# Summing a dense expert sweep in eights: eight keys per PSUM bank instead of four, on one core

## What is computed

```python
# 512 tokens; 16384 experts = 128 x 128 keys; 8 heads x 16 experts per token
act = gelu(einsum('td,ted->te', h, u_emb[expert])) * gate
out = einsum('te,ted->td', act, v_emb[expert])      # d = 2048
y   = rmsnorm(x + ga2 * out, g_final)
```

## Time and profile before

| what | value |
|---|---|
| runs of the kernel before | 3456.78, 3446.84, 3457.04 us; median 3456.78 us |
| span of the profiled execution | 3458.3 us (no other time is given for it) |
| PE, DVE, ACT, POOL busy over the span | 98%, 68%, 29%, 52% |
| chain that ended last | PE 88%, DVE 7%, the rest 5% |
| granted TensorE clock, mean | 0.990 of full speed |
| evictions `acc<-acc,bank` (L1962) | 372, 251.5 us busy |

### The profile page before, as it was taken

How to read it: one execution, slowest core, us unless ns; L and a number is a source line. 1 busy time by engine, 2 the same in 40 slices (tenths; PEclk the granted TensorE clock), 3 DMA queues, 4 the chain that set the end, 5 groups by cost and what they waited for, 6 DMA issues and landing times.

```text
span 3458.3 us, 44792 instructions
## 1 busy us (share of the span) xinstructions
PE 3376.2 (98%) x16931; PEld 2936.1 (85%) x16931; DVE 2361.7 (68%) x3848; ACT 1012.7 (29%) x1160; POOL 1805.8 (52%) x904
## 2 busy tenths in 40 slices
PE   6999999999999999999999999999999999999998
PEld 3688888766788889999999999999888888888886
DVE  2278887755514659994888888764667776767666
ACT  3332211143223232223222222223333323233233
POOL 1220000212544446676666666667777777778764
PEclk8999999999999999999999999999999999999999
DMA  8656642564424226777677777788988888888872
GB/s 337 265 186 205 216 168 94 191 245 175 194 96 152 90 105 248 265 278 275 257 314 302 281 282 299 305 314 313 377 327 329 317 325 328 316 326 324 321 277 97
DMA packets 184619, 874.72 MB, mean 253 GB/s; under 512 B 16621, under 2 KB 77501, under 8 KB 97844
## 3 DMA queue, kind: packets, MB, share of 16 engines
q1 hardware_dynamic: 122160, 525.38, 42.0%
q0 software_dynamic: 38688, 281.15, 20.1%
q10 hardware_dynamic: 23652, 66.69, 5.1%
HBM read 803.78 MB, written 69.32 MB: 252 GB/s over the span
## 4 chain that ended last, share of the span: by engine, by line
PE 88%; DVE 7%; DMA 1%; POOL 1%; issue 1%; ACT 1%; ACTq 0%; DVEq 0%; SPq 0%; POOLq 0%
PE bank L2080 82%; PE bank L2336 2%; PE bank L2452 1%; DMA ring<-in_w_mod 1%; PE bank L2310 1%; DVE b L1845 1%; PE bank L2088 1%; POOL low L769 1%; DVE rows_a L1784 1%; DVE b L1825 0%; DVE rows_c L1784 0%; PE bank L2436 0%; DVE tiny L1840 0%; DVE rows_b L1784 0%; DVE low L1403 0%
## 5 line engine op out<-in xcount | busy, mean ns | idle before, releaser
L811 POOL TENSOR_TENSOR split<-ring,split 128x1024 fp32r<-128x1024 f32 x544 | 1303.9, 2410 | 542.4 <-ACT split L1146 540.4
L2080 PE MATMUL bank<-h_hi,split 128*128 128x384 f32 (+1 forms) x4608 | 1221.8, 341 | 8.3 <-POOL split L811 7.0
L1146 ACT ACTIVATE split<-ring 128x1024 fp32r<-128x1024 f32 x544 | 577.8, 1063 | 1608.7 <-PE bank L2080 1588.3
L2080 PE MATMUL bank<-split,a_split 128*128 128x512 f32 x4608 | 1045.0, 389 | 0.1
L2080 PEld LDWEIGHTS bank<-split,a_split 128*128 128x128 f32 x4608 | 865.1, 188 | 179.8 <-POOL split L811 0.5
L2080 PEld LDWEIGHTS bank<-h_hi,split 128*128 128x128 f32 x4608 | 839.7, 188 | 29.7 <-POOL split L811 8.9
L2080 PE MATMUL bank<-h_lo,split 128*128 128x384 f32 (+1 forms) x2304 | 785.5, 341 | 0.0
L1962 DVE TENSOR_TENSOR acc<-acc,bank 128x512 f32<-128x512 f32 x372 | 251.5, 683 | 289.7 <-PE bank L2080 288.7
L2080 PEld LDWEIGHTS bank<-h_lo,split 128*128 128x128 f32 x2304 | 433.6, 188 | 9.5
L2080 PE MATMUL bank<-hT_hi,w_hi 128*128 128x512 f32 (+1 forms) x768 | 290.5, 378 | 8.5 <-DVE hT_lo L1408 4.4
L2080 PE MATMUL bank<-hT_lo,w_hi 128*128 128x512 f32 (+1 forms) x768 | 288.2, 375 | 0.0
(11 more groups left out here) (315 smaller groups left out, 3787.3 us busy)
## 6 DMA issues: line engine op xcount, KB each, us to landing
ring<-in_u_emb SPq DMA_DIRECT2D x128, 1024.0 KB
ring<-in_v_emb SPq DMA_DIRECT2D x128, 1024.0 KB
ring<-in_w_mod SPq DMA_DIRECT2D x48, 1024.0 KB
ring<-in_w_in SPq DMA_DIRECT2D x44, 1024.0 KB
ring<-in_w_mod SPq DMA_DIRECT2D x64, 512.0 KB, 4.7
neurons<-tiny ACTq DMA_DIRECT2D x128, 192.0 KB
gate_table<-b ACTq DMA_DIRECT2D x6, 4096.0 KB, 14.7
weigh<-neurons SPq DMA_DIRECT2D x32, 768.0 KB
```

The lines of the kernel that those rows point to most:

```text
L811: nc.gpsimd.tensor_tensor(split[:, r % 2, 1, at].bitcast(F32R), ring[:, r % 4, :, :].rearrange("p k n -> p (k n)")[:, at], split[:, r % 2, ...
L1146: nc.scalar.activation(split[:, q % 2, 0, at].bitcast(F32R), ring[:, q, :, :].rearrange("p k n -> p (k n)")[:, at], ACT.Copy)\
L2080: last = mm(out_, left[a].bitcast(F32R), right[b].bitcast(F32R), start=start and n == 0, stop=stop and n == 2)
```

## The change

A unit's place in the order changes: eight units now are two key groups by four column quarters, unit = 8i + k, group 2i + k % 2, quarter k // 2. A bank is begun by the even unit and finished by the odd one, with 24 matmuls, so DVE empties it only in odd units (192 flushes and merges instead of 384 of them). Both places of `a_split` are now read in turn in all eight units. ACT makes the first one of the next eight after unit 6 and the second after unit 7, and DVE's `rest_group` stands at the head of units 7 and 0; `weigh_group` stands in units 5 and 6. SP's two weigh loads stand ahead of units 2 and 4, each behind a wait for the `rest_group` of the place's old group. In the first eight units groups 2 and 3 are loaded ahead of units 4 and 6. Two small tensors of the row-by-row part (`h2_last`, `nval_last`) move to other places in SBUF.

```diff
@@ SyncE
-            def v_load(unit, group, q):
+            def v_load(unit, group, k):
                 sp.wait_ge(split_made, unit * 2 + 2 * (V0 - 3))
-                sp.dma_start(ring[:, q, :, :].rearrange("p k n -> p (k n)"),
-                             v_t[bass.ds(group, 1), q, :, :].rearrange("g p n -> p (g n)"))\
-                  .then_inc(quarter_full[q], 16)
+                sp.dma_start(ring[:, k % 4, :, :].rearrange("p k n -> p (k n)"),
+                             v_t[bass.ds(group, 1), k // 2, :, :].rearrange("g p n -> p (g n)"))\
+                  .then_inc(quarter_full[k % 4], 16)
...
-                    if k == 2 and not first:
-                        sp.wait_ge(a_split_made, i * 2)
-                        weigh_load(i * 2 + 1, 1)
-                    if k == 6 and not last:
-                        sp.wait_ge(a_split_made, i * 2 + 1)
-                        weigh_load(i * 2 + 2, 0)
-                    v_load(i * 8 + k, i * 2 + k // 4, k % 4)
+                    if k in (2, 4) and not last:
+                        sp.wait_ge(a_split_made, i * 2 + k // 2)
+                        weigh_load(i * 2 + 1 + k // 2, k // 2 - 1)
+                    v_load(i * 8 + k, i * 2 + k % 2, k)
...
             for k in range(4, 8):
-                if k == 6:
-                    sp.wait_ge(a_split_made, 1)
-                    weigh_load(2, 0)
-                v_load(k, 1, k % 4)
+                if k % 2 == 0:
+                    sp.wait_ge(a_split_made, k // 2 - 1)
+                    weigh_load(k // 2, k // 2 - 2)
+                v_load(k, k % 2, k)
@@ ScalarE
-                if k == NK - 2:
-                    a_hi(0, 0)
+                if k >= NK - 2:
+                    a_hi(k - NK + 2, k - NK + 2)
                 neurons(k, k % 4)
...
             with act.Fori(1, GROUPS // 2 - 1) as i:
                 for k in range(8):
+                    if k == 0:
+                        a_hi(1, i * 2 + 1)
+                    if k == 7:
+                        a_hi(0, i * 2 + 2)
                     sweep_unit(i * 8 + k, k % 4)
-                    if k % 4 == 1:
-                        a_hi((k // 4 + 1) % 2, i * 2 + (k // 4 + 1))
@@ VectorE (full_bank, flush and merge count pairs of units)
+            def flush_here(unit, j):
+                if unit % 2:
+                    (merge if unit >= NK - 8 else flush)(unit // 2, j)
+
             weigh_group(0)
             dot(NK - 5)
             rest_group(0)
+            weigh_group(1)
             dot(NK - 4)
+            rest_group(1)
             rows_added = 0
             for unit in range(NK):
-                g = unit // 4
-                flush_here = merge if g == GROUPS - 1 else flush
+                g, k = unit // 8 * 2, unit % 8
+                if k == 7 and g + 2 < GROUPS:
+                    rest_group(g + 2)
+                if k == 0 and g:
+                    rest_group(g + 1)
                 flush_here(unit, 0)
-                if unit % 4 == 0 and g + 1 < GROUPS:
-                    weigh_group(g + 1)
+                if k in (5, 6) and g + 2 < GROUPS:
+                    weigh_group(g + k - 3)
...
                 flush_here(unit, 1)
-                if unit % 4 == 2 and g + 1 < GROUPS:
-                    rest_group(g + 1)
@@ TensorE
-            def sums(unit, k, a_count, first=False):
-
-                pe.wait_ge(a_split_made, a_count)
-                s = k // 4 % 2
+            def sums(i, k, first=False):
+
+                unit, s = i * 8 + k, k % 2
+                pe.wait_ge(a_split_made, i * 2 + (s + 1))
                 for j in range(JD):
-                    o = JD * k + j
+                    o = JD * (k // 2) + j
...
-                    elif not first or o > 3:
-                        pe.wait_ge(sum_free, unit * JD + (j - 3))
+                    elif s == 0 and (not first or o > 3):
+                        pe.wait_ge(sum_free, i * (4 * JD) + (o - 3))
...
-                                   [split[:, k % 2, h, a * NB:(a + 1) * NB] for h in range(2)], a == 0, a == GROUP - 1)
+                                   [split[:, k % 2, h, a * NB:(a + 1) * NB] for h in range(2)],
+                                   s == 0 and a == 0, s == 1 and a == GROUP - 1)
...
-                    if j < JD - 1:
+                    if s == 1 and j < JD - 1:
                         last.then_inc(sum_full, 1)
```

More of the change, by code:

```diff
@@ L206, in hybrid_layer @@
             expT = region("expT", 2 * TD, tables)[:, :].rearrange("p (w t) -> p w t", w=2)
-            h2_last = region("h2_last", P, tables)[:, :]
-            nval_last = region("nval_last", P, tables)[:, :]
         with ExitStack() as gather:
@@ L294, in hybrid_layer @@
         act_s = small[:, 1792:1920]
+        h2_last = small[:, 1920:2048]
+        nval_last = tiny[:, 2720:2848]
         ga2_part = [small[:, i * NB:(i + 1) * NB] for i in range(3)] + [ga2_last]
@@ L654, in weigh_load, with sweep_loads @@
                   .then_inc(weigh_full[s], 16)
-            def sweep_loads(i, first=False, last=False):
+            def sweep_loads(i, last=False):
                 for k in range(8):
@@ L675, in _ @@
             for k in range(4):
-                v_load(k, 0, k)
+                v_load(k, k % 2, k)
             for b in range(2):
@@ L1314, in _ @@
             for k in range(8):
+                if k == 7:
+                    a_hi(0, 2)
                 sweep_unit(k, k % 4)
-                if k % 4 == 1:
-                    a_hi((k // 4 + 1) % 2, k // 4 + 1)
                 if k == 0:
@@ L1334, in _ @@
                 for k in range(8):
+                    if k == 0:
+                        a_hi(1, i * 2 + 1)
+                    if k == 7:
+                        a_hi(0, i * 2 + 2)
                     sweep_unit(i * 8 + k, k % 4)
-                    if k % 4 == 1:
-                        a_hi((k // 4 + 1) % 2, i * 2 + (k // 4 + 1))
             for k in range(6):
+                if k == 0:
+                    a_hi(1, GROUPS - 1)
                 sweep_unit(NK - 8 + k, k % 4)
-                if k == 1:
-                    a_hi(1, GROUPS - 1)
                 if k == 2:
@@ L1944, in rest_group, with full_bank, flush, merge @@
                                         a_split[:, g % 2, 0, :, :], ALU.subtract).then_inc(a_split_made, 1)
-            def full_bank(unit, j):
+            def full_bank(pair, j):
                 if j < JD - 1:
-                    dve.wait_ge(sum_full, 2 * unit + j + 1)
+                    dve.wait_ge(sum_full, 2 * pair + j + 1)
                 else:
[L1951 to L1958, removed]
+                    dve.wait_ge(split_used, 2 * (V0 + 2 * pair + 1) + 2)
+                return bank[:, 4 + (JD * pair + j) % 4, :]
+            def flush(pair, j):
+                src = full_bank(pair, j)
+                part = acc[:, j, (pair % 4) * NB:(pair % 4 + 1) * NB]
+                if pair < 4:
                     nc.vector.tensor_copy(part, src).then_inc(sum_free, 1)
                     return
-                dve.wait_ge(sum_free, JD * (unit - 4) + j + 1)
+                dve.wait_ge(sum_free, JD * (pair - 4) + j + 1)
                 nc.vector.tensor_tensor(part, part, src, ALU.add).then_inc(sum_free, 1)
-            def merge(unit, j):
-                q = unit % 4
+            def merge(pair, j):
+                q = pair % 4
                 o = JD * q + j
                 part = acc[:, j, q * NB:(q + 1) * NB]
-                flush(unit, j)
-                dve.wait_ge(sum_free, JD * unit + j + 1)
+                flush(pair, j)
+                dve.wait_ge(sum_free, JD * pair + j + 1)
                 nc.vector.tensor_tensor(part, part, ga2_part[q], ALU.mult).then_inc(merge_step, 1)
@@ L2521, in sums @@
                                    [a_split[:, s, h, a, j * P:(j + 1) * P] for h in range(2)],
-                                   [split[:, k % 2, h, a * NB:(a + 1) * NB] for h in range(2)], a == 0, a == GROUP - 1)
+                                   [split[:, k % 2, h, a * NB:(a + 1) * NB] for h in range(2)],
+                                   s == 0 and a == 0, s == 1 and a == GROUP - 1)
                         if j == JD - 1 and a % 2:
                             last.then_inc(split_used, 1)
-                    if j < JD - 1:
+                    if s == 1 and j < JD - 1:
                         last.then_inc(sum_full, 1)
             for k in range(8):
-                sums(k, k, k // 4 + 1, True)
+                sums(0, k, True)
             with pe.Fori(1, GROUPS // 2) as i:
                 for k in range(8):
-                    sums(i * 8 + k, k, i * 2 + (k // 4 + 1))
+                    sums(i, k)
 _INS = ['x', 'c', 'ctx', 'c_ctx', 'w_mod', 'b_mod', 'g_mix', 'g_ffn', 'w_in', 'w_gate', 'b_gate', 'g_mhn', 'conv_w',
```

## The result

The changed kernel takes 3465.68 us (median of seven runs, 3460.23 to 3470.66), the kernel before 3449.33 us in its runs to date (seven, 3446.84 to 3463.27). The ratio is 1.0038 with a 95% interval of 1.0025 to 1.0051: about 13 us slower, 9 to 18. So, by the middle of that interval, it fell on the "slower" side, which had 0.26, with the time inside the range and 5.4 us above the number. The profiled execution took 3464.41 us, with a span of 3462.6.

The account below looks back on a forecast made before the run. PE was taken to bound the sweep and DVE the 15.7 us behind it. Tail -3.2, start 2.0 + 0.7 and hold 4 gave +3.5 on the median 3456.8: 3460.3 us; forecast's own range 3454 to 3469, overall 3449 to 3480.

Parts of the forecast that it names:

- slower: Outcome side: the kernel slower by over 10.4 us, about 0.3%; chance 0.26.
- the forecast's upper end: Top of the forecast's own range, all terms at their costly ends: +12 us, 3469 us.
- PE's work: Sweep: the same 4608 matmuls, 192 fewer bank openings worth at most 21 us, taken as 0.
- evictions: DVE in the sweep: 192 fewer at 0.684 us take 131 us off DVE, all cover, worth 0.
- SP's hold: SP's queue waits ahead of weigh and ring loads, making unit 2 late: about 4 us, between 0 and 15.
- The tail: Behind PE's last matmul: DVE's last eviction starts 3.2 us earlier, so -3.2 us.
- The start: Near unit 4, landing behind a weigh load: 2.0 us lost, plus 0.7 of slow clock.
- The left operand: Making `a_split` later: ready at 6.15 us, PE wants it at 8.03; hidden with 1.9 to spare, costs 0.
- a rival with a chance of 0.10 and 7 us: Left operand late at 28 places x 0.3 x 0.8, POOL having waited for DVE's added rows: some 7 us more, 3467; chance 0.10.
- The prediction's own signs of being wrong: Other matmul spacing than 0.2268 us, PE waiting on DVE's `a_split` or an eviction, or granted clock under full speed mid-sweep.
- The first rival: SP's hold stops PE in every pair of groups: 14 x (1.1 to 4.9), +15 to +69, middle 3490; chance 0.18.
- Faster: Faster by over 0.3%, PE's own rate gaining from longer sums, 1% of each matmul or 21 us; chance 0.07.

Follow-up runs that it names:

- e6_evict: Changed kernel with start ring units first, weigh loads two units later, row adds at unit heads, plus an unread bank reduction per eviction from fifth pair: 3453.29 us, 0.9997.
- e2_hold: Changed kernel with SyncE's two weigh loads in the loop ahead of units 4 and 6 of each eight instead of 2 and 4: 3462.78 us, 1.0036.
- e5_quarters: Changed kernel with GpSimd making each half of the split in two instructions of 512 columns instead of one of 1024: 3471.39 us, 1.0050.

## Why the prediction was right and wrong

**The number: in part luck.** The forecast of +3.5 us was added to 3456.78, the median of three runs; seven put the kernel before at 3449.33. So the time lies 5.4 us above the number, while the change cost 13 us by the ratio and 16.5 in the two stages, beyond the +12 of the forecast's upper end.

**PE's work, evictions: right.** Shortest and median matmul are unchanged, and the 131 us of evictions were cover, as e6_evict shows from the other side.

**SP's hold: right in mechanism, its size by luck.** The sum had 4 us; measured 3.8, at units 10, 50, 98 and 106, each of the form 8i + 2 as worked out, and gone in e2_hold. Its spread was not foreseen: 4 of 14 places, not half of them at half a lateness, and 2.6 of the 3.8 us stand at one, unit 10.

**The tail: right.** -3.2 was the sum, -3.3 was measured. The last eviction (answering to rows 11) in VectorE's order of time:

```profile
3452.14 0.68 DVE L1961 TENSOR_TENSOR acc<-acc,bank 128x512 f32<-128x512 f32 x1
```

That is 1.9 us behind PE's end at 3450.2, where 2.05 was worked out.

**The start: right mechanism, mis-sized.** 2.0 of lateness and 0.7 of clock stood in the sum; the profile shows 5.8. Unit 4's landing was put 30.1 us behind the sweep's begin. ScalarE shows it 32.0 behind (2417.15 - 2385.2):

```profile
2417.15 2.00 ACT L1143 ACTIVATE split<-ring 128x1024 fp32r<-128x1024 f32 x2 [14.30 <-DMA ring<-in_v_emb]
```

PE's idle time is 2.7 us, and the half clock behind it takes another 2.6 and some at its edges. The like stall of rows 10 had cost 1.4 us of clock, and I took half. What made unit 4 late is in the DMA view of the same stretch, from 14.1 us behind the sweep's begin (2399.3) to ScalarE's row (queue, packets, MB, share):

```profile
DMA packets 2087, 7.27 MB, mean 408 GB/s; under 512 B 112, under 2 KB 1392, under 8 KB 1392
...
q1 hardware_dynamic: 1557, 3.45, 51.2%
q0 software_dynamic: 288, 2.10, 28.3%
q10 hardware_dynamic: 241, 1.71, 23.0%
```

Gathers and x are about as in the sum (2.10 and 1.71 MB). SP's own queue moved 3.45 MB, not the 2.65 of the weigh load and unit 4, but the 0.8 MB more are packets of unit 5, issued behind unit 4. A load lands in 16 parts: by the trace 15 of unit 4's had landed at 2415.48, 30.3 us behind the sweep's begin and so about where the sum had them, and the last at 2417.12. So 1.6 of the 1.9 us by which the landing was missed are one straggling part. The last parts of the loads next to it straggled by 1.0 to 2.0 us; why is not shown. The Trainium skill, DMA: Bandwidth & Descriptors, § Where 436 GB/s comes from, gives 358 GB/s for one core; by it the landing would have been at 32.7 us, an estimate. That lies nearer, but for another reason: 408 moved here over 18 us.

**The left operand: the step that failed.** "It is hidden with 1.9 us to spare, at both places, and costs 0." It costs 9.5 us, the largest term of all, at units 17, 33, 73 and 89. The step began POOL's two halves as ACT's first copy was done, 0.25 us ahead of its second. That is true only if POOL is there. In the kernel after, POOL stood in front of its gather until DVE had added a row, 5.36 us in the row at 2659.41, and its halves ended 8.4 us behind the beginning of ACT's second copy (2665.14 - 2656.75), not 4.5. They held DVE's subtraction until 1.6 us behind their end, and PE stopped for 2.03 us. DVE thus waits for POOL that has waited for DVE. POOL's lateness also decides how long: it found both copies made, the case in which DVE waited for both halves every time. The same chain with a wait of 2.90 us stands ahead of unit 17:

```profile
2527.03 6.57 DVE L1941 TENSOR_TENSOR a_split<-weigh,a_split 128x1536 fp32r<-128x1536 f32 x1 [0.43 <-ACT a_split L1297]
...
2526.29 0.94 POOL L828 DMA_INDIRECT rows_a<-in_v_rows,small  x1 [2.90 <-DVE bank L1993]
2527.25 4.74 POOL L808 TENSOR_TENSOR split<-ring,split 128x1024 fp32r<-128x1024 f32 x2
```

All of this was written down as a rival with a chance of 0.10 and 7 us. The chain was right and its price near, but not its shape: four places with waits of 1.1 to 2.5 us and slow clock on top, not 28 x 0.3 of 0.8. They lie 56 units apart, 17 and 73, 33 and 89, for eight rows are gathered and added in seven units and a pair of groups takes eight; ahead of units 33 and 89 DVE adds two rows in one unit, 31 and 87. The chance was the mistake: the 39 waits of POOL could be read from the trace before, and they should have moved the step itself. The prediction's own signs of being wrong came with it: PE waited on DVE's `a_split`, and behind unit 89's stop the granted clock was 0.71 from 3129.2 to 3135.0. Before the change the same waits were there, more of them, and cost nothing: one left operand was made in four units, and PE wanted it two units after the copy.

With its own terms measured the sum reads -3.3 + 5.8 + 3.8 + 9.5 + 0.8 = +16.6 (0.8 for the small rest beyond that of before), and the two stages say +16.5. The forecast's sum, +3.5, was short mainly by the left operand, which it put at nothing, and by the start's missing 3.1.

**The first rival** (a hold that stops PE in every pair) did not come: 4 places of 14. Its "middle" of 3490 was wrong by its own terms, since +15 to +69 has its middle at +42, some 3499; nothing else rests on it. **Faster** did not come, and the matmul's unchanged minimum says why.

The Trainium skill, SBUF — State Buffer, § Who interferes with whom, has issue order decide which of VectorE and GpSimd waits for the port pair that they share. Taken one instruction at a time, as the prediction took it, that would have put DVE's subtraction between POOL's instructions, and the left operand on time. The trace agrees at 2509.61 and does not at 2662.11, nor in e5_quarters at 2667.79, where the subtraction began in the second of POOL's four instructions and waited for the third and the fourth too.

## What to carry to other kernels

When work is moved to a later point, take the slack of each engine that it needs from its waits in the trace, not from the order in the code alone: here POOL's 39 waits for DVE, harmless before, ate a margin of 1.9 us. A wait on a queue in order is paid by what stands behind it; putting the held load two units later gave back all of the ring's cost. And a stall of PE can be dearer than its gap: at the start the stretch at half clock behind it cost as much again.

## What had not been expected of the hardware

- In the row at 2527.03 DVE's subtraction starts 0.22 us before POOL's halves and still ends at 2533.60, 1.6 us behind their end at 2531.99, after 6.57 us where it takes 1.75 alone. POOL was then already in the gather's instruction (2526.29 to 2527.23) ahead of its halves. At 2593.94, likewise beside such an instruction but 0.74 us before the halves, a subtraction took 1.76 us, so a start shortly before them is not always enough.
- POOL's instruction that issues a gather takes 0.96 us in the median, and 2.30 in some; ahead of unit 17's stop, one of 2.30 us at 2521.09 runs beside DVE's subtraction of 2518.87 to 2522.55. All 33 such long ones in the sweep of the kernel after began during an operation of DVE on `weigh`, and none of the 96 short ones did.
- The stages ahead of the sweep, the same in the kernel after and in every experiment but e5_quarters, end anywhere between 2384.7 and 2400.0 us. Their spread of 15 us is as large as the effect that was studied.
